# Splitting the attention output projection into two halves, and setting its feeding steps to later beats

## What is computed

```python
for l in range(DEPTH):
    h = rms_norm(x, norm1_g[l])
    q, k, v, gu, gv = jnp.split(h @ w_in[l], splits, axis=-1)
    q = apply_rope(rms_norm(q, q_norm_g[l]), cos, sin)
    k = apply_rope(rms_norm(k, k_norm_g[l]), cos, sin)
    attn = banded_window_attention(q, k, v, sink[l])
    sgu = chunked_spatial_gating(gelu(gu), gelu(gv), sgu_ln_g[l], sgu_ln_b[l], w_s[l], b_s[l])
    mixed = concatenate([rms_norm(attn, attn_out_g[l]), rms_norm(sgu, sgu_out_g[l])])
    x = x + mixed @ w_o[l]
    x = x + conv_gated_ffn(rms_norm(x, norm2_g[l]), ...)
```

## Time and profile before

| | before |
|---|---|
| median of 3 runs (lowest to highest) | 3592.89 us (3592.19 to 3593.06) |
| profiled execution, own time | 3593.61 us |
| its span | 3591.7 us |
| PE busy | 3489.6 us (97%) |
| DVE, ACT, POOL busy | 2729.6, 1891.9, 1689.4 us (76, 53, 47%) |
| mean granted TensorE clock | 0.991 of full speed |
| data by DMA | 624.37 MB, mean 174 GB/s |

### The profile page before, as it was taken

One profiled execution on the slowest core, in us unless ns is written; L12 is line 12 of the kernel. 1 busy time (PEld: TensorE's weight loads), 2 busy tenths in 40 slices (PEclk: granted clock), 3 DMA queues, 4 the chain that ended last, 5 costly groups with the idle time before them and its releaser, 6 DMA issues.

```text
span 3591.7 us, 52952 instructions
## 1 busy us (share of the span) xinstructions
PE 3489.6 (97%) x19584; PEld 3001.1 (84%) x19584; DVE 2729.6 (76%) x4035; ACT 1891.9 (53%) x2857; POOL 1689.4 (47%) x1473
## 2 busy tenths in 40 slices
PE   8998999999999999998999999999998999999999
PEld 7887788888887888886888888888886888888888
DVE  8768886679899976776788758877676788658875
ACT  6554785455555554765444434444765544434443
POOL 4324672167877822143366406653143466306640
PEclk9999999999999999999999999999998999999999
DMA  5544556655555556543555665566543555665566
GB/s 192 168 156 140 162 182 186 188 180 170 176 169 166 178 165 188 178 132 111 186 188 187 184 189 187 186 185 188 173 134 110 186 188 187 184 191 185 187 185 179
DMA packets 177041, 624.37 MB, mean 174 GB/s; under 512 B 19784, under 2 KB 25616, under 8 KB 175760
## 3 DMA queue, kind: packets, MB, share of 16 engines
q1 hardware_dynamic: 171216, 606.11, 53.7%
q10 hardware_dynamic: 5568, 14.89, 1.2%
HBM read 618.75 MB, written 2.17 MB: 173 GB/s over the span
## 4 chain that ended last, share of the span: by engine, by line
PE 71%; DVE 10%; POOL 5%; ACT 3%; issue 3%; DMA 0%; ACTq 0%; POOLq 0%; DVEq 0%
PE psG L524 43%; PE psG L522 23%; DVE WL L1266 3%; PE psG L521 2%; POOL SQ L1725 1%; ACT WH L761 1%; DVE sdx L1279 1%; POOL SQ L1744 1%; ACT L781 1%; POOL sdx L1727 1%; PE psM L547 1%; DVE Et L1528 1%; DVE Et L1535 0%; POOL GV L1866 0%; DVE Y L1271 0%
## 5 line engine op out<-in xcount | busy, mean ns | idle before, releaser
L524 PE MATMUL psG<-H,WH 128*128 128x512 f32 x5655 | 2025.9, 398 | 0.0
L1266 DVE TENSOR_TENSOR WL<-RAW,WH 128x1024 fp32r<-128x1024 f32 (+1 forms) x1162 | 1496.0, 1287 | 552.7 <-ACT WH L761 550.8
L761 ACT ACTIVATE WH<-RAW 128x1024 fp32r<-128x1024 f32 (+1 forms) x1162 | 1214.8, 1045 | 952.3 <-PE psG L524 932.5
L522 PE MATMUL psG<-H,WL 128*128 128x256 f32 x6032 | 1667.2, 287 | 0.1
L524 PEld LDWEIGHTS psG<-H,WH 128*128 128x128 f32 x5655 | 1068.5, 189 | 234.1
L522 PEld LDWEIGHTS psG<-H,WL 128*128 128x128 f32 x6032 | 1146.1, 190 | 45.3 <-issue 9.6
L524 PE MATMUL psG<-Y,WH 128*128 128x512 f32 x2816 | 998.6, 398 | 0.0
L522 PE MATMUL psG<-Y,WL 128*128 128x256 f32 x2944 | 807.5, 281 | 11.6 <-DVE Y L1273 10.6
L524 PEld LDWEIGHTS psG<-Y,WH 128*128 128x128 f32 x2816 | 530.4, 188 | 122.1
L522 PEld LDWEIGHTS psG<-Y,WL 128*128 128x128 f32 x2944 | 557.0, 189 | 26.0 <-DVE WL L1266 11.2
L1875 POOL TENSOR_SCALAR fou<-fsu,PAR 128x256 f32<-128x256 f32 x88 | 177.9, 2022 | 565.3 <-DVE fsu L1308 565.3
(11 more groups left out here) (350 smaller groups left out, 3578.9 us busy)
## 6 DMA issues: line engine op xcount, KB each, us to landing
RAW<-in_w_up SPq DMA_DIRECT2D x352, 512.0 KB, 3.6
RAW<-in_w_o_in SPq DMA_DIRECT2D x162, 512.0 KB, 3.6
RAW<-in_w_e_in SPq DMA_DIRECT2D x128, 512.0 KB, 3.6
RAW<-in_w_down SPq DMA_DIRECT2D x128, 512.0 KB, 3.5
RAW<-in_w_in SPq DMA_DIRECT2D x112, 512.0 KB, 3.6
RAW<-in_w_o SPq DMA_DIRECT2D x72, 512.0 KB, 3.6
RAW<-in_w_e_out SPq DMA_DIRECT2D x64, 512.0 KB, 4.3
RAW<-in_w_o_out SPq DMA_DIRECT2D x64, 512.0 KB, 4.2
```

What stands on the lines that cost most here:

```text
L522: ins = e.matmul(o[:, 0:T], wl, x[:, 0:T], start=False, stop=False, skip_group_check=True)
L524: ins = e.matmul(o, wh, x, start=False, stop=last)
L761: copy = lambda o, i, scale=1.0: e.activation(o, i, ACT.Copy, scale=scale)
L1266: tt(WL_[c % NRAW][:, 0:n], RAW_[c % NRAW][:, 0:n], WH_[c % NW][:, 0:n].bitcast(F32), SUB).then_inc(sem("wl"), 1)
```

## The change

Twelve of the 16 output tiles of the attention product are split. Twelve jobs of a new kind `ra` take the attention chunk alone, and each is added to X when it is done; then twelve `res` jobs take the gating chunk; then come four whole tiles. The gating half is so first read 24 beats after the start. Each part has its own PSUM bank in the rotation, and each ends with two additions to X on DVE. The chunks and their bytes are the same.

```diff
+SPLIT = 12
...
-                        self.end[j] = b + (kind != "res")
+                        self.end[j] = b + (kind not in ("res", "ra"))
...
-        out("res", 2 + 3 * l, lambda n: I["w_o2"][l * 16 + n], y_(2 + l, range(16)))
+
+        for n in range(SPLIT):
+            S.group(("ra", l * SPLIT + n, I["w_o2"][l * 16 + n][:, 0:CH * P], y_(2 + l, range(8))))
+        for n in range(SPLIT):
+            S.group(("res", (2 + 3 * l) * 16 + n, I["w_o2"][l * 16 + n][:, CH * P:], y_(2 + l, range(8, 16))))
+        for n in range(SPLIT, 16):
+            S.group(("res", (2 + 3 * l) * 16 + n, I["w_o2"][l * 16 + n], y_(2 + l, range(16))))
...
-        S.event("attn", l, S.end_of("Q", l * 8 + 7) + 26)
+        S.event("attn", l, S.end_of("Q", l * 8 + 7) + 32)
         for i in range(8):
-            S.event("sgt", l * 8 + i, s0 + 18 + i)
-            S.event("sgm", l * 8 + i, max(S.end_of("gu", l * 8 + i) + (8 if i < 7 else 4), s0 + 22 + i))
+            S.event("sgt", l * 8 + i, s0 + 21 + i * 5 // 4)
+            S.event("sgm", l * 8 + i, max(S.end_of("gu", l * 8 + i) + 7, s0 + 30 + i))
...
+            for a in at("ra", b - 1):
+                x = X[a % SPLIT]
+                w.wait_ge(sem("big"), S.done("ra", a))
+                own.up(tt(x, out_of("ra", a), x, ADD))
+                w.wait_ge(own.sem, own.n)
+                tt(x, out_2("ra", a), x, ADD).then_inc(sem("ra"), 1)
```

More of the change, by code:

```diff
@@ L431, in build @@
             evac.append((sem("res"), i + 1))
+        elif kind == "ra":
+            evac.append((sem("ra"), i + 1))
         else:
@@ L679, in attention @@
             for kind in ("K", "Q"):
-                for i in at(kind, b - 9):
+                for i in at(kind, b - 10):
                     a = qk_n(kind, i)
@@ L691, in attention @@
                 ready(use, ins)
-            for i in at("Q", b - 14):
+            for i in at("Q", b - 18):
                 a, g = qk_n("Q", i), i % 8 // 4
@@ L697, in attention @@
                     ready(use, e.matmul(use.ap[:, 0:T], qs[a % 4][:, r * P:(r + 1) * P], KK[g], start=True, stop=True))
-            for i in at("Q", b - 19):
+            for i in at("Q", b - 25):
                 use = take(("pt", i))
@@ L705, in attention @@
                 ready(use, ins)
-            for i in at("Q", b - 22):
+            for i in at("Q", b - 29):
                 use = take(("pv", i))
@@ L724, in gating @@
                         sums(("mu", l), i, GV[i], 8)
-                for l in at("sgu", b - 10 - k):
+                for l in at("sgu", b - 12 - k):
                     for i in (2 * k, 2 * k + 1):
@@ L734, in gating @@
                 ready(use, ins)
-            for u in at("sgt", b - 2):
+            for u in at("sgt", b - 4):
                 use = take(("gw", u))
@@ L1156, in attention @@
                 copy(VV[i % 2], use.ap[:, 0:T]).then_inc(use.sem, 1)
-            for i in at("Q", b - 16):
+            for i in at("Q", b - 20):
                 l, hd = divmod(i, 8)
@@ L1165, in attention @@
                 ins.then_inc(sem("a_exp"), 1)
-            for i in at("Q", b - 20):
+            for i in at("Q", b - 26):
                 use = small[("pt", i)]
@@ L1172, in attention @@
                 copy(apt[i % 2 * 2 + 1], use.ap[:, T:2 * T]).then_inc(use.sem, 1)
-            for i in at("Q", b - 23):
+            for i in at("Q", b - 30):
                 use = small[("pv", i)]
@@ L1202, in gating @@
                         e.activation(gq[i % 4], GV[i], ACT.Square).then_inc(sem("gv_sq"), 1)
-            for l in at("sgu", b - 14):
+            for l in at("sgu", b - 16):
                 w.wait_ge(sem("gu_n"), 8 * l)
@@ L1219, in gating @@
             for i in range(8):
-                for u in at("sgm", b - 3 - i // 4):
+                for u in at("sgm", b - 5 - i // 2):
                     if u % 8 == 7:
@@ L1316, in evictions @@
                 w.wait_ge(sem("big"), S.done("res", r))
+                if n < SPLIT and r // 16 in (2, 5):
+                    w.wait_ge(sem("ra"), r // 48 * SPLIT + n + 1)
                 own.up(tt(X[n], out_of("res", r), X[n], ADD))
@@ L1563, in attention @@
             for kind in ("K", "Q"):
-                for i in at(kind, b - 10):
+                for i in at(kind, b - 11):
                     a = qk_n(kind, i)
@@ L1570, in attention @@
             for kind in ("K", "Q"):
-                for i in at(kind, b - 12):
+                for i in at(kind, b - 14):
                     a = qk_n(kind, i)
@@ L1576, in attention @@
                     tt(KK[i % 2] if kind == "K" else qs[a % 4], qs[a % 4], qq[a % 4], ADD).then_inc(sem("q_rope"), 1)
-            for i in at("Q", b - 15):
+            for i in at("Q", b - 19):
                 l, hd = divmod(i, 8)
@@ L1592, in attention @@
                     ts(c[r][1], c[r][0], par(f"pc{l}", "sink", hd), -1.0, MAX, MUL).then_inc(sem("a_max"), 1)
-            for i in at("Q", b - 17):
+            for i in at("Q", b - 22):
                 c = [[sm_[i % 2 * 2 + r][:, j:j + 1] for j in range(8)] for r in range(2)]
@@ L1628, in gating @@
             for k in range(4):
-                for l in at("sgu", b - 15 - k):
+                for l in at("sgu", b - 17 - k):
                     w.wait_ge(sem("gv_rms"), l + 1)
@@ L1634, in gating @@
                         stt(GV[i], GV[i], h5[:, i:i + 1], gr, MUL, MUL).then_inc(sem("gv_n"), 1)
-            for u in at("sgt", b - 3):
+            for u in at("sgt", b - 5):
                 l, i = divmod(u, 8)
@@ L1647, in gating @@
             for i in range(8):
-                for u in at("sgm", b - 2 - i // 4):
+                for u in at("sgm", b - 4 - i // 2):
                     if u % 8 == 7:
@@ L1653, in gating @@
                         stt(GU[i], GU[i], par(f"pc{l}", "sog", i), gr, MUL, MUL).then_inc(sem("gu_n"), 1)
-                for u in at("sgm", b - 3 - i // 4):
+                for u in at("sgm", b - 6 - i // 2):
                     if u % 8 == 7:
@@ L1827, in attention @@
             for kind in ("K", "Q"):
-                for i in at(kind, b - 11):
+                for i in at(kind, b - 12):
                     a = qk_n(kind, i)
@@ L1843, in attention @@
                     tt(t, t, s, MUL).then_inc(sem("g_poly"), 1)
-            for i in at("Q", b - 24):
+            for i in at("Q", b - 31):
                 l, k = divmod(i, 8)
@@ L1861, in attention @@
             for k in range(4):
-                for l in at("sgu", b - 16 - k):
+                for l in at("sgu", b - 18 - k):
                     w.wait_ge(sem(f"pc{l}"), 16)
```

## The result

The changed kernel takes 3543.55 us in the median of four runs (3540.86 to 3545.83), the one before in the same comparison 3592.85: the ratio is 0.9863, 95% interval 0.9852 to 0.9875. The forecast was 3555 us, so the change gained 49.3 us where 37.6 were forecast.

A forecast was written before the change was run, and what follows sets the result against it. PE bounds the feed-forward; the two attention layers lose PE time to waits and slow clock. Gains 6.8 + 4.5 + 1.4 + 6.1 = 18.8 us a layer, 37.6 for both: 3593.6 to 3556.0, median 3555 us; range 3535 to 3580.

The forecast's parts named there:

- heads, idle time: Attention heads: one more beat before `qr` and `pv` ends PE's waits for scaled q and `apt`; gain 6.8 us a layer.
- gq, idle time: PE's wait for the squares gq: moving `attn` 6 beats removes 3.5 of 5.1 us a layer; 1.6 stay.
- gating copies, idle time: PE's waits for copies of transposed gating tiles: 4.8 of 6.2 us stay, gain 1.4 us a layer.
- Y, idle time: PE's wait for the gating half's low part in the output product: 5.3 us shrinks by 4.8 a layer.
- clock: PE's slow clock after waits: 1.0 us behind gq and 1.3 behind Y come back in each layer.
- The wait takes a new place: Gating product: POOL's eight biases and two polynomials delay the tile 2 copy behind a tanh; PE waits 4.3 us at `gw`.
- What is added: Split output tiles: 24 more DVE additions to X a layer, 10.2 us, hide in the `ra` chunks and cost nothing.
- the rows show both stretched: Output product: POOL's SS additions (1.60 us) and DVE's low part of H (0.77) slow each other instead of excluding each other.
- the rival of POOL and DVE in turn: Twelve split tiles: the two engines exclude each other, 4.2 us against a 2.82 us chunk; 10 us a layer, 3575 us, chance 0.08.
- So a layer holds 25.9 + 3.6 = 29.5 us that an order of steps could give back, both 59 us.: Attention layers: 25.9 us without PE work plus 3.6 of slow clock, costed in the first layer and doubled.
- The clock loss stays: Slow clock behind the wait for gating copies, priced at 1.3 us a layer, was expected to remain.
- The rival of clear copies: Gating copies arrive with a 0.2 us wait since POOL runs at faster prices; 12 us more gain, 3543 us, chance 0.25.

The follow-up runs named there:

- at beat 33: Changed kernel with odd gating biases on DVE and attention steps at beat 33 for 32: 3541.93 us; with tanh and gelu product also later, 3539.16 us.
- the split alone: Kernel before with only the twelve-tile output split, every other step at its old beat: 3586.06 us, ratio 0.9983.
- the 16 tiles: Changed kernel with all 16 output tiles split instead of twelve: 3545.26 us, ratio 0.9866.
- the later gelu and the biases halved: Changed kernel with tanh and gelu product 5 beats after their job instead of 3, and four odd gating biases on DVE instead of POOL: 3542.88 us.
- the kernel with the copies first: Changed kernel with ACT's copies of transposed gating tiles ahead of the gelu's tanh in each beat: 3543.82 us, ratio 0.9861.

## Why the prediction was right, and where its number was off

In us, both layers:

| term | forecast | measured |
|---|---|---|
| heads, idle time | 13.6 | 13.0 |
| gq, idle time | 7.0 | 8.0 |
| gating copies, idle time | 2.8 | 2.4 |
| Y, idle time | 9.6 | 10.6 |
| other idle time | 0 | 1.3 |
| clock | 4.6 | 8.9 |
| PE's busy time at full clock | 0 | 4.3 |
| sum | 37.6 | 48.5 |

The four named idle terms were right to 1.0 us each, 33.0 forecast and 34.0 measured. The waits that they name before and after give these numbers; the other 1.3 is what is left of the 35.3.

- *Heads.* One beat was enough for `apt`. The new wait for `ax` and, in the second layer, one for the scaled q make 0.4 and 1.2 us, where 0.5 a layer was left for collisions.
- *Squares gq.* 1.1 us stay where 1.6 were forecast, by the forecast's cause: at beat 33 they go.
- *Gating copies.* "The wait takes a new place" is what happened, behind the ten POOL steps, 15.3 us long. The copies came later than the count had them, since the first bias stood 7.5 us behind the last sums of gq (1632.72 - 1625.19) and not 5.9. The experiments add what the prediction did not see: it is a ring. Loosen ACT's order, and the wait moves to another bank of PE or to DVE; loosen POOL, and it waits for DVE.
- *Gating half.* Forecast 17.6 us from the beat of the root to the last low part. Measured 15.7 from ACT's `split_hi` at 1677.02, so nothing stays where 0.5 was left. `split_lo` took 1.22 us and not 1.35, and DVE's steps overlap a little, which the sum by means leaves out: four scalings in a row took 1.67 us (the split alone, above) and not 4 x 0.48 = 1.92.
- *What is added.* 24 additions a layer cost nothing that can be seen: no wait for WL, with twelve tiles or 16. DVE's busy time rose by 8.6 us and not by some 20 (2729.6 to 2738.2): the additions to X took 20.4 more in the two layers, but other steps took less, the low parts of H by 6.4. And "the rows show both stretched" misread POOL's 1.60 us, as the 16 tiles show; the rival of POOL and DVE in turn counted a wait as work.

The step that was mis-sized is the clock: "So a layer holds 25.9 + 3.6 = 29.5 us that an order of steps could give back, both 59 us." It took two 4 us stretches and gave Y the price of another wait. In 1 us windows the first layer lost 5.2 us, 1.5 behind gq, 1.7 behind the gating copy and 2.0 behind Y, because the half clock outlasted the stretches; and the second lost 7.0 behind the same waits (2.3, 2.8 and 2.0), so doubling one layer was wrong for this term. "The clock loss stays" for the gating copies held in the first layer, 1.7 us before and after; in the second it went from 2.8 to 1.6, there behind the wait at the transposition.

The other missing piece, 4.3 us of busy time, was no term at all. It goes with the new beats of the heads: over all runs the first layer has 292.0 to 293.3 us with them and 294.4 to 294.7 without, the second 291.3 to 292.9 and 293.5 to 293.8. Part of it shows just after a wait: there the group of `gw` takes 0.71 us (the earlier trace rows and the row of L750 above) and 0.61 without one, and those of `pv` and `qr` before the change 1.10 and 0.67 against 1.03 and 0.59. Eleven waits fewer in the first layer's list would make about 1 of its 2.4 us by that, an estimate. The rest stays open.

The rival of clear copies gave the right time by luck: its 12 us were to come from the gating copies, which gave 2.4 in all, and came from clock and busy time.

## To carry to other kernels

Price the clock behind each stall from windows of 1 us, in each place and each repetition by itself, until the granted clock is full again; a window chosen by eye cuts it off. Count short waits on a saturated engine with a little more than their idle time (about 0.1 us each here). Before a long step is priced as work beside another engine, see whether it ends a fixed time behind that engine's step. Where four engines feed each other in a ring, moving one step in one list moves the wait to the next engine; look for the engine without gaps (here DVE) before planning another order.

## What was not expected of the hardware

The length of a stall does not tell by itself whether the clock falls. In the changed kernel PE waits 2.42 us for the same POOL bias in both layers. In the first the matmuls behind that wait took their usual 0.39 us; in the second, after its end at 2687.29, three windows stand at the low level or near it:

```profile
2688.00:2689.00 1.00, 1.00 (x4) 0.84 (x4) 0.96 (x3) 0.39 (x2) 1.00 (x2) 0.50 0.02 8
2689.00:2690.00 1.00, 1.00 (x5) 0.87 (x4) 1.00 (x1) 0.00 (x0) 1.00 (x2) 0.50 0.00 0
2690.00:2691.00 1.00, 1.00 (x6) 0.82 (x6) 0.97 (x2) 0.00 (x0) 1.00 (x2) 0.67 0.00 0
```

With the later gelu and the biases halved, PE stood 3.27 us for DVE's bias, until 1652.23, and then ran at full clock:

```profile
1652.00:1653.00 1.00, 0.77 (x5) 0.74 (x6) 0.96 (x4) 0.00 (x0) 0.77 (x2) 1.00 0.01 4
```

In the kernel with the copies first, the same wait for POOL, 2.41 us, did cost 1.7 us in the first layer; and the wait of 3.8 us for the gating copy cost 1.7 us in one layer of the kernel before and 2.8 in the other. So a stall of 2 to 4 us cost from 0 to 2.8 us of clock here, and no run tells beforehand which.

POOL's bias steps do not have one price. In the changed kernel (number, then shortest, median and longest in ns):

```profile
L1883 POOL TENSOR_SCALAR GV<-GV,PAR x16: 919/1236/2192, 1632.7 to 2692.2; 128x256 f32<-128x256 f32 x16
```

Eight of the 16 had no `split_lo` beside them for more than 0.25 us and took 0.92 to 1.03 us; the eight with one took 1.44 to 2.19, as this one of DVE and POOL:

```profile
1633.65 1.22 DVE L1275 TENSOR_TENSOR WL<-RAW,WH 128x1024 fp32r<-128x1024 f32 x1
1633.72 2.19 POOL L1883 TENSOR_SCALAR GV<-GV,PAR 128x256 f32<-128x256 f32 x1
```

The means of six in a row (8.14 / 6 and 9.43 / 6) hide this. With half of the biases on DVE, POOL's took 1.0 to 1.1 us each.
